# Two-layer encoder on one core: norm 2 and layer 1's first norm computed by token, and the router with tokens stationary

## What is computed

```python
def encoder_layer(x, c, ...):
    shift1, scale1, gate1, shift2, scale2, gate2 = split(silu(c) @ w_ada + b_ada, 6)
    h = rms_norm(x, norm_attn) * (1 + scale1) + shift1       # "first norm"
    proj = h @ w_in                                          # two attention mixers, gates
    ...
    x = x + gate1 * merged
    h2 = rms_norm(x, norm_ffn) * (1 + scale2) + shift2       # "norm 2"
    x = x + gate2 * grouped_moe(h2, w_router, ...)           # 16 experts, top 2
    return x

def rms_norm(x, g):
    return x * rsqrt(mean(x * x, axis=-1) + EPS) * g

# in grouped_moe
    scores = sigmoid(t @ w_router)     # (512 tokens, 16 experts), then top 2 of the best group of 4
```

## Time and profile before

| | us |
|---|---|
| median of 3 runs | 1721.64 |
| lowest, highest | 1717.2, 1724.36 |
| profiled execution | 1720.92 |
| its span, first to last instruction | 1719.1 |

### The profile page before, as it was taken

The page is one execution under the profiler, slowest core; times in us unless marked ns, Lnnn a source line. Parts: engine busy times, 40 slices in busy tenths (PEclk is TensorE's granted clock), DMA queues, the critical chain, the costliest instruction groups (busy, mean ns, idle before and its releaser), DMA issues.

```text
span 1719.1 us, 19087 instructions
## 1 busy us (share of the span) xinstructions
PE 1464.2 (85%) x6598; PEld 1090.4 (63%) x6598; DVE 1068.3 (62%) x1371; ACT 883.0 (51%) x1194; POOL 141.8 (8%) x149
## 2 busy tenths in 40 slices
PE   3799987999956999999769999699997499999982
PEld 2477545787725777777537664378874377777772
DVE  1464469433467888888373725963344678888876
ACT  3531458323235777777363324752233377777764
POOL 1000000000001112221000000000000102222213
PEclk9899998999977999999889999899998699999996
DMA  9532660112227999999772247201132689999943
GB/s 299 193 109 87 231 211 1 50 49 96 101 98 274 358 363 344 360 326 350 265 218 98 75 144 256 66 29 70 49 105 92 244 302 345 354 349 331 348 177 150
DMA packets 163247, 342.29 MB, mean 199 GB/s; under 512 B 25070, under 2 KB 27264, under 8 KB 163056
## 3 DMA queue, kind: packets, MB, share of 16 engines
q1 hardware_dynamic: 151472, 317.21, 52.4%
q0 software_dynamic: 10992, 23.43, 3.8%
q10 hardware_dynamic: 720, 0.84, 0.2%
HBM read 334.10 MB, written 24.12 MB: 208 GB/s over the span
## 4 chain that ended last, share of the span: by engine, by line
PE 54%; DVE 14%; DMA 13%; issue 9%; ACT 7%; POOLq 2%; SPq 0%; ACTq 0%; DVEq 0%; PEldq 0%; PEld 0%
PE bank L732 10%; PE bank L734 10%; PE bank L733 10%; DMA y_by_choice<-zone,row_now 6%; DMA zone<-rows_by_token,row_now 5%; PE bank L763 2%; PE bank L900 2%; PE bank L1030 2%; PE bank L1032 2%; PE bank L1031 2%; PE bank L922 2%; PE bank L1015 2%; PE bank L1016 2%; PE bank L1017 2%; DVE w_lo L2055 2%
## 5 line engine op out<-in xcount | busy, mean ns | idle before, releaser
L732 PE MATMUL bank<-x_hi,w_lo 128*128 128x512 f32 x608 | 246.2, 405 | 27.9 <-DVE x_lo L1595 17.1
L734 PE MATMUL bank<-x_hi,w_hi 128*128 128x512 f32 x608 | 239.0, 393 | 0.0
L733 PE MATMUL bank<-x_lo,w_hi 128*128 128x512 f32 x608 | 238.7, 393 | 0.0
L2055 DVE TENSOR_TENSOR w_lo<-ring,zone_r 128x2048 fp32r<-128x2048 f32 x92 | 210.3, 2291 | 27.7 <-ACT zone_r L1400 27.7
L1400 ACT CAST x_lo<-ring 128x2048 fp32r<-128x2048 f32 x96 | 183.8, 1916 | 62.2 <-PE bank L1017 24.9
L1400 ACT CAST zone_r<-ring 128x2048 fp32r<-128x2048 f32 x96 | 182.8, 1911 | 24.6 <-PE bank L1032 13.9
L1015 PE MATMUL bank<-w_lo,zone_r 128*128 128x512 f32 x384 | 157.4, 410 | 5.5 <-issue 5.5
L1572 DVE TENSOR_TENSOR w_lo<-ring,w_hi 128x1024 fp32r<-128x1024 f32 x84 | 102.6, 1221 | 87.4 <-ACT w_hi L1164 86.8
L732 PEld LDWEIGHTS bank<-x_hi,w_lo 128*128 128x128 f32 x608 | 114.9, 189 | 65.0 <-issue 25.9
L733 PEld LDWEIGHTS bank<-x_lo,w_hi 128*128 128x128 f32 x608 | 115.4, 190 | 25.3 <-issue 2.4
L734 PEld LDWEIGHTS bank<-x_hi,w_hi 128*128 128x128 f32 x608 | 115.2, 190 | 25.2
(11 more groups left out here) (286 smaller groups left out, 2831.8 us busy)
## 6 DMA issues: line engine op xcount, KB each, us to landing
ring<-in_w_gate SPq DMA_DIRECT2D x32, 2048.0 KB, 13.5
ring<-in_w_up SPq DMA_DIRECT2D x32, 2048.0 KB, 13.9
ring<-in_w_down SPq DMA_DIRECT2D x32, 2048.0 KB, 8.7
ring<-in_w_ada SPq DMA_DIRECT2D x24, 2048.0 KB, 8.9
ring<-in_w_in SPq DMA_DIRECT2D x14, 2048.0 KB, 8.4
ring<-in_w_out SPq DMA_DIRECT2D x4, 2048.0 KB, 7.9
zone<-y_by_choice SPq DMA_DIRECT2D x8, 1024.0 KB, 8.0
ring<-in_w_in SPq DMA_DIRECT2D x16, 256.0 KB, 5.2
```

The source lines that it names most:

```text
L732: mm(out, lo, x_first, start=start, stop=False)
L733: mm(out, hi, x_second, start=False, stop=False)
L734: return mm(out, hi, x_first, start=False, stop=stop)
L2055: v.tensor_tensor(w_low[EXPERT_SLOTS[par][k]][:, cols], ring[EXPERT_SLOTS[par][k]][:, cols], part_hi[buf].bitcast(F32), ALU.subtract)\
```

## The change

Both norms are computed by token. TensorE gets the squares as the stationary side, 128 tokens at a time, and one column of ones as the moving side; the result is one sum for each token, 128 x 4. Root and reciprocal work on these four columns. VectorE writes the factors as four diagonal blocks (identity times factor, into `tmp[:, 1, :]`), TensorE multiplies the ones with them, and so each factor stands on all partitions again, in PSUM under the key `("rms", which)`. The products read it there, and the bank is freed when all of them are done. In norm 2 the squares are still added over the chunks first; in layer 1's first norm each chunk's squares go to TensorE as before. The router has 128 tokens of `hT` stationary and the 16 columns of `w_rout` moving, so its result has tokens on the partitions; the copy of the logits and the four transposes are gone.

```diff
+            def token_sums(use, which, chunks):
+                ps = take(use, ("sumsq", which))
+                for c, (sem_, count, src) in enumerate(chunks):
+                    pe.wait_ge(S[sem_], count)
+                    for t in range(TT):
+                        ins = mm(ps[:, t:t + 1], src[:, t * P:(t + 1) * P], K("ones")[:, 0:1],
+                                 start=(c == 0 and (t == 0 or len(chunks) == 1)),
+                                 stop=(c == len(chunks) - 1 and (t == TT - 1 or len(chunks) == 1)))
+                done(use, ("sumsq", which), ins)
+
+            def spread_factors(use, which):
+                ps = take(use, ("rms", which))
+                pe.wait_ge(S["tok_diag_ready"], TT * (which + (1 if use is layer_uses_of[1][0] else 0)))
+                for t in range(TT):
+                    ins = mm(ps[:, t * P:(t + 1) * P], K("ones"), tok_diag[:, t, :], start=True, stop=True)
+                done(use, ("rms", which), ins)
...
                     elif what == "squares":
-                        back_squares(layer_use, 0)
+                        token_sums(layer_use, 0, [("sq_ready", c + 1, hT[:, c, :]) for c in range(KC)])
+                        spread_factors(layer_use, 0)
...
-                sumsq(layer_use, ("sumsq", 1), 1)
-                ps = take(layer_use, "router")
+                token_sums(layer_use, 1, [("sumsq_ready", 1, tmp[:, 0, :])])
+                spread_factors(layer_use, 1)
+                ps = take(layer_use, "scores")
                 for k in range(KC):
                     wait_h(pe, k)
-                    ins = mm(ps[0:NE, :], w_rout[:, k, :], hT[:, k, :], start=(k == 0), stop=(k == KC - 1))
-                done(layer_use, "router", ins)
-                ps = take(layer_use, "scores")
-                pe.wait_ge(S["logits_ready"], 1)
-                for t in range(TT):
-                    ins = nc.tensor.transpose(ps[:, t * NE:(t + 1) * NE], logits[:, t * P:(t + 1) * P],
-                                              K("ident", NE)[:, 0:NE])
+                    for t in range(TT):
+                        ins = mm(ps[:, t * NE:(t + 1) * NE], hT[:, k, t * P:(t + 1) * P], w_rout[:, k, :],
+                                 start=(k == 0 and t == 0), stop=(k == KC - 1 and t == TT - 1))
                 done(layer_use, "scores", ins)
...
             def norm_root(use, which):
                 ps = wait_full(act, use, ("sumsq", which))
-                freed(af(root[:, 0, :], ps[:, :], ACT.Sqrt, bias=eps[:, 0:1], scale=1.0 / D), use, ("sumsq", which))
+                freed(af(four[:, 2, :], ps[:, 0:TT], ACT.Sqrt, bias=eps[:, 0:1], scale=1.0 / D), use, ("sumsq", which))
...
                 norm_shift()
-                ps = wait_full(act, use, "router")
-                nc.scalar.copy(logits, ps[0:NE, :]).then_inc(S["logits_ready"], 1)
-                act.wait_ge(S["logits_ready"], 1)
-                nc.scalar.sem_inc(free[use["router"][0]], 1)
                 ps = wait_full(act, use, "scores")
...
             def norm_rstd(own, use, which):
                 b, n = use[("sumsq", which)]
                 dve.wait_ge(free[b], n + 1)
-                own.step(v.reciprocal(rstd[:, :], root[:, 0, :]))
-                own.last()
+                own.step(v.reciprocal(four[:, 3, :], four[:, 2, :]))
+                own.last()
+                for t in range(TT):
+                    v.tensor_scalar(tok_diag[:, t, :], K("ident"), four[:, 3, t:t + 1], None, ALU.mult)\
+                        .then_inc(S["tok_diag_ready"], 1)
+                return wait_full(dve, use, ("rms", which))
...
-                    norm_rstd(own, use, 0)
+                    factors = norm_rstd(own, use, 0)
                 low_part(0)
                 for c in range(KC + 2):
                     if c < KC:
-                        norm_scale(c)
+                        norm_scale(c, factors)
+                    if layer and c == KC:
+                        dve.wait_ge(S["xn_ready"], KC)
+                        v.sem_inc(free[use[("rms", 0)][0]], 1)
...
-                norm_rstd(own, use, 1)
-                norm_apply(own)
+                norm_apply(own, norm_rstd(own, use, 1))
+                dve.wait_ge(S["xn_ready"], KC + len(SHIFT_ACT))
+                v.sem_inc(free[use[("rms", 1)][0]], 1)
```

More of the change, by code:

```diff
@@ L274, in layer_uses @@
                 yield ("bias", h), (0, 1, 2, 3)
-        elif what in ("rms", "squares"):
+        elif what == "rms":
+            yield ("rms", 0), (0,)
+        elif what == "squares":
             yield ("sumsq", 0), (0,)
+            yield ("rms", 0), (2,)
         else:
@@ L301, in layer_uses @@
     yield ("sumsq", 1), (3,)
-    yield "router", (0,)
+    yield ("rms", 1), (2,)
     yield "scores", (1,)
@@ L447, in build_trunk @@
         pick = part(10848, 128).rearrange("p (i t e) -> p i t e", i=2, t=TT)
-        logits = zone[0:NE, 12288:12288 + TOK]
+        tok_diag = tmp[:, 1, :].rearrange("p (t n) -> p t n", t=TT)
         gw = sb("gw", [P, 2, TT])
@@ L478, in build_trunk @@
                  "oa_ready", "ob_raw", "got_weighed", "mix_ready", "ob_ready", "gate_ready", "m_ready", "br_hi_ready", "br_lo_ready",
-                 "o_hi_ready", "o_lo_ready", "logits_ready", "score_ready",
+                 "o_hi_ready", "o_lo_ready", "tok_diag_ready", "score_ready",
                  "rows_ready", "pick_ready", "map_ready", "index_ready",
@@ L791, in rms_wide @@
             def rms_wide():
-                ps = take(layer_use, ("sumsq", 0))
+                ps = take(layer_use, ("rms", 0))
                 pe.wait_ge(x_diag_ready, TT)
@@ L796, in rms_wide @@
                     ins = mm(ps[:, t * P:(t + 1) * P], K("ones"), x_diag[:, t, :], start=True, stop=True)
-                done(layer_use, ("sumsq", 0), ins)
+                done(layer_use, ("rms", 0), ins)
             def back(use, nth):
@@ L812, in back @@
                             done(use, ("back", c), ins)
[L814 to L819, removed]
             for layer in range(DEPTH):
@@ L1573, in low_part, with norm_scale @@
                                 w_hi[:, n % W_BUFS, :, :].bitcast(F32), ALU.subtract).then_inc(S["w_lo_ready"], 1)
-            def norm_scale(c):
+            def norm_scale(c, rstd):
                 if c not in SCALE_DVE:
@@ L1597, in norm_low, with norm_apply @@
                 ins.then_inc(S["x_lo_ready"], 1)
-            def norm_apply(own):
+            def norm_apply(own, rstd):
                 for c in range(KC):
@@ L1678, in _ @@
                         freed(v.tensor_copy(xT[:, c, :], ps[:, :]), use, ("back", c))
-                    ps = wait_full(dve, use, ("sumsq", 0))
+                    ps = wait_full(dve, use, ("rms", 0))
                     own.step(v.tensor_copy(rstd[:, :], ps[:, :]))
                     own.last()
-                    v.sem_inc(free[use[("sumsq", 0)][0]], 1)
+                    v.sem_inc(free[use[("rms", 0)][0]], 1)
+                    factors = rstd
                     for c in range(1, KC, 2):
```

## The result

The changed kernel took 1728.7 us (median of 6 runs, 1725.8 to 1729.92) beside 1721.39 us for the kernel before (6 runs): a ratio of 1.0037, 95% interval [1.0022, 1.0051]. I had forecast 1715.8 us, 0.34% down; it went 0.37% up. The profiled execution of after took 1725.8 us (span 1724.0) against 1720.92 (span 1719.1) of before, 4.9 us more.

What follows compares the result with a forecast made beforehand. TensorE was busy for 85% of the span, but the touched stretches were bound by serial waits. Norm 2 and router, -4.5 us, and first norm, -1.3, gave -5.8: 1715.1 profiled, 1715.8 us as median; range 1710 to 1731.

Steps and rivals of the forecast that it cites:

- Part 1: Norm 2's token sums: eight records take 1.5 us against 1.56 removed, no gain; bounds 0.5 gain, 0.3 loss.
- Part 2: Norm 2, end of sums to first product: 3.43 us instead of 4.13, gain 0.7, or 1.4 with the clock up.
- Part 3: Router: 64 load-bound records take 8.9 us instead of 8.56, the clock rising some 3.3 us in; cost 0.4 us.
- Part 4: Router's end to sigmoid: 0.03 us remain of 1.99, the table load running before the router ends; gain 1.95.
- Part 5: Layer 1's first norm: sums cost 0.1 us more, sums to scaling gains 1.45, so -1.3 us with the clock up.
- A: Rival: the clock doesn't count narrow-column work; routers take 14.3 us, total +9.2, about 1731 us; chance 0.25.
- B: Rival: clock warmer than assumed, up throughout, router at its floor; -10, 1711.6 us; chance 0.1.
- C: Rival: sigmoid's table load stays behind the router, or something later takes what was won; about 1719 us; chance 0.12.
- The experts' start moves with the sigmoid: Norm 2 to experts: a microsecond saved before the sigmoid is one off the whole, as experts wait for it.
- The sum: Whole kernel: -4.5 us for two layers' norm 2 and router, -1.3 for layer 1's first norm, -5.8 in all.
- floor: Router: can't end before its last activations arrive, 6.4 us after its start, plus 1.1 for their records; 7.5 us.

Runs made afterwards that it cites:

- warm_narrow: Changed kernel with 128 moving columns in token sums, 16 in the router, and unread products in TensorE's waits of both norms: 1709.78 us, ratio 0.994 to the kernel before.
- after_hot: Changed kernel as it is (1 and 16 moving columns), plus unread products in TensorE's waits of both norms and the plan: 1712.55 us, ratio 0.9941 to the kernel before.

## Why the prediction was wrong, point by point

- **Part 1, token sums.** Right. Taken 1.5 us, measured 1.35 (1.63 in layer 1, where it was 1.76). The prices of 0.11 and 0.22 us a record held (0.11 over 874.4 to 877.9; 0.21 over the router).
- **Part 2, root to first product.** Right in its terms: root 0.27, reciprocal 0.19, four diagonal products 0.88, hand-over 0.14, spread 2.06 at the lower clock. The sum was 3.43 and measured 3.63, a gain of 0.5. Reading the factors from PSUM cost nothing: the whole-row products took 0.680 us on the mean, 0.685 before.
- **Part 3, the router.** This step failed. I let the clock rise "some 3.3 us after the start, as now", taken over from a router of 512 moving columns. Under 16 it never rose: 13.8 us in place of 8.9, +4.9 a layer. With 128 columns, and so with the clock's rise that I had assumed, the router took 9.15.
  The Trainium skill's page "TensorE: Matmul & The Clock Gate", section "LDWEIGHTS (loading the stationary operand)", gives a load as its columns over 1.2, so 107 ns for 128 columns, and sets no other figure for the other level of the clock. At the upper clock the trace agrees (0.11 us a record), at the lower it doesn't (13.40 us for 63).
- **Part 4, router to sigmoid.** Right: 0.03 us remain where 1.99 were. The sigmoid's table load ran at 491.54, while the router was still busy for 7 us:

```profile
491.54 1.28 ACT L1385 ACT_TABLE_LOAD   x1
499.03 0.22 ACT L1385 ACTIVATE zone<-bank 128x64 f32<-128x64 f32 x1 [6.20 <-PE bank L975]
```

- **Part 5, the first norm.** Failed for the same reason. I wrote "the clock being up" and took it to stay up: 10.31 us in place of 7.2, spread 2.05 in place of 1.16, scaling 2.7 us later in place of 1.3 earlier, and 0.8 us more from QKV's first matmul to the next norm 2 (QKV had the lower clock for its first 12.8 us, 8.8 before).
- **The rivals.** A is what happened, in its mechanism and nearly in its sizes: router 13.8 us (14.3 was its figure), +2.6 and +2.9 us from the sums' start to the sigmoid in the two layers (it had +3.15), +2.7 in the first norm (+2.9). Its total of 1731 lies 2.3 us above the median (the edited stretches lost 8.2 us in the trace, where it had 9.2). I gave it 0.25. The one row of such work, the map matmul, spoke for it; that the old router had needed 3.1 us as well was evidence about a router of 512 columns, not about this one. B and C did not occur: the clock was colder, and the table load is hidden.
- **The experts' start moves with the sigmoid.** Right in direction; 2.35 of the 2.6 us arrived in layer 0 and 2.27 of the 2.9 in layer 1. In layer 0's chain the ranks' two matmuls, which now found the clock up, took 0.65 us in place of 1.10, and some of that was lost again behind the map.
- **The sum.** The -5.8 us failed by the clock's course. wide_both, which has the change's operations with 128 moving columns and no fillers, came out 7.5 us under the kernel before (ratio 0.996 [0.9945, 0.9976]); its trace is 6.1 us shorter over the two ways from the sums to the experts and the way from the first norm's sums to QKV. With the clock up for both kernels the prediction's own terms give -1.4 for root to first product, nothing for two routers at their floor and -1.95 behind them, so -3.35 a layer, and -1.3 in the first norm: -8.0, beside -7.7 measured.

## What to carry to other kernels

Turning a matmul around so that activations become the stationary operand trades moving columns for loads, and at 1 or 16 moving columns TensorE is busy without gap while its clock behaves as if it were idle (no such stream with between 24 and 128 columns was run). Before such a change look at the granted clock over a stretch of the same shape (here 16 records with 24 columns at 0.50), and if the loads bind anyway, let more columns move behind them: 128 in place of 16 cost nothing (0.21 us a record at the lower clock and 0.11 at the upper with either) and took the router from 13.8 to 9.15 us. TensorE's waits of a few microseconds can be filled with products that nobody reads, which gave 0.7% on the kernel before and as much on the widened change (ratio 0.996 to 0.9892), but each filler stands in the queue ahead of real work and must end before its wait does. Before pricing one part by its records alone, look when its last input comes: the old router at the upper clock was held to 7.6 us by that, not by its records alone.

## What the runs showed of the hardware that I had not expected

- The granted clock fell from 1.00 to 0.50 while TensorE's row was full: at 878 in the changed kernel's first norm (32 records in 3.5 us, then 33 in 6.65), and in the routers of warm_narrow and after_hot. With 128 columns behind the same loads it stayed at 1.00 for all 64 records (7.20 us).
- From the lower level, 64 loads with 16 columns left it at 0.50 for 13.4 us, and 3.6 us of the f32 transposes behind them brought it up. So transposes of whole f32 blocks brought it up, where the narrow stream had not.
- A record of 512 columns of whole f32 takes 0.44 us at the upper clock (16 in 7.10), one of fp32r 0.23 (the output projection of before starts one every 0.227 us from 469.75 to 475.42), and TensorE's rows name both f32: the type stands only in the rows of the engines that wrote the operands.
